# Branch projections in three rounded passes, branch by branch, and a first expert tile in fp32

## The reference

```python
# h: normalised and modulated tokens; gates: the last 3 * 1024 columns of h @ w_in
g_f, g_g, g_d = jnp.split(jax.nn.sigmoid(gates), N_BRANCHES, axis=-1)
merged = (g_f * (fourier_mix(u_f) @ w_f)      # w_fourier (512, 1024)
          + g_g * (o_g @ w_go)                # w_gqa_o   (512, 1024)
          + g_d * (o_d @ w_do))               # w_diff_o  (512, 1024)
x = x + g1 * (merged @ w_out)
...
# moe: 16 experts, two per token; t: tokens after the second norm
gate = jnp.einsum('td,edf->tef', t, w_gate_l)
up = jnp.einsum('td,edf->tef', t, w_up_l)
act = jax.nn.silu(gate) * up * combine[..., None]
x = x + g2 * jnp.einsum('tef,efd->td', act, w_down_l)
```

## Time and profile before

| | |
|---|---|
| median of 3 runs | 2156.6 us (2156.22 to 2162.78) |
| the profiled execution, its own time | 2155.64 us |
| its span, first to last instruction | 2153.8 us, 30419 instructions |
| granted TensorE clock, mean | 0.964 |
| TensorE matmul | 1965.9 us busy, 91% of the span |
| TensorE weight load (beside it) | 1611.4 us, 75% |
| VectorE | 1025.5 us, 48% |
| ScalarE | 850.0 us, 39% |
| GpSimd | 340.8 us, 16% |
| DMA | 336.28 MB, 156 GB/s on average |

### The profile page before, as it was taken

How to read it: one execution, slowest core, us unless ns; L and a number is a source line. 1 busy time by engine, 2 the same in 40 slices (tenths; PEclk the granted TensorE clock), 3 DMA queues, 4 the chain that set the end, 5 groups by cost and what they waited for, 6 DMA issues and landing times. The chain is left out here.

```text
span 2153.8 us, 30419 instructions
## 1 busy us (share of the span) xinstructions
PE 1965.9 (91%) x12363; PEld 1611.4 (75%) x12363; DVE 1025.5 (48%) x1718; ACT 850.0 (39%) x1377; POOL 340.8 (16%) x131
## 2 busy tenths in 40 slices
PE   6999899999999969999679997878999998799994
PEld 5889766688888856676478995657888887677673
DVE  5384367511122266777564733672221123677763
ACT  4333455511111235565334334654111123366553
POOL 1223000013222220000222221000222230200003
PEclk9999999999999989999889998999999999899997
DMA  7312378628211159899431220001212112899954
GB/s 268 107 59 61 129 245 262 209 88 303 88 59 56 58 200 342 305 313 313 168 114 41 69 70 31 2 1 51 77 59 88 59 45 98 322 408 389 313 204 170
DMA packets 163853, 336.28 MB, mean 156 GB/s; under 512 B 10370, under 2 KB 121602, under 8 KB 149252
## 3 DMA queue, kind: packets, MB, share of 16 engines
q1 hardware_dynamic: 151488, 299.63, 40.1%
q0 software_dynamic: 5760, 20.97, 2.6%
q10 hardware_dynamic: 6468, 13.74, 1.8%
HBM read 334.58 MB, written 53.74 MB: 180 GB/s over the span
## 5 line engine op out<-in xcount | busy, mean ns | idle before, releaser
L653 POOL TENSOR_TENSOR wlo<-raw,whi 128x2048 fp32r<-128x2048 f32 x50 | 230.4, 4608 | 1075.5 <-ACT whi L676 1075.5
L1729 DVE TENSOR_TENSOR xw_gu_lo<-xw_gu_raw,xw_gu_hi 128x2048 fp32r<-128x2048 f32 x100 | 228.0, 2283 | 26.7 <-ACT xw_gu_hi L1515 26.6
L170 PE MATMUL psum<-h_hi,whi 128*128 128x320 f32 x896 | 217.1, 324 | 20.4 <-DVE h_lo L155 17.7
L170 PE MATMUL psum<-whi,h_hi 128*128 128x256 f32 x720 | 212.4, 295 | 0.0
L170 PE MATMUL psum<-wlo,h_hi 128*128 128x256 f32 x720 | 206.2, 286 | 0.0
L170 PE MATMUL psum<-whi,h_lo 128*128 128x256 f32 x720 | 206.2, 286 | 0.0
L170 PE MATMUL psum<-h_lo,whi 128*128 128x320 f32 x896 | 205.2, 310 | 0.0
L170 PE MATMUL psum<-h_hi,wlo 128*128 128x320 f32 x896 | 205.0, 310 | 0.0
L833 ACT ACTIVATE sig_m<-psum 128x640 f32<-128x640 f32 x48 | 33.8, 705 | 400.0 <-PE psum L170 400.0
L1515 ACT ACTIVATE xw_gu_hi<-xw_gu_raw 128x2048 fp32r<-128x2048 f32 x100 | 185.5, 1907 | 0.0
L1868 PE MATMUL psum<-xw_d_raw,act_T 128*128 128x512 f32 x400 | 179.9, 592 | 0.9 <-ACT act_T L1541 0.9
(11 more groups left out here) (288 smaller groups left out, 3463.4 us busy)
## 6 DMA issues: line engine op xcount, KB each, us to landing
xw_gu_raw<-w_e_gate SPq DMA_DIRECT2D x50, 1024.0 KB
xw_gu_raw<-w_e_up SPq DMA_DIRECT2D x50, 1024.0 KB
xw_d_raw<-w_e_down SPq DMA_DIRECT2D x50, 1024.0 KB, 9.8
raw<-w_in SPq DMA_DIRECT2D x46, 1024.0 KB, 5.4
wm_rest<-w_mod SPq DMA_DIRECT2D x40, 1024.0 KB, 5.2
y_rows<-y_sel SPq DMA_DIRECT2D x50, 512.0 KB, 9.6
h_sel<-h_rows SPq DMA_DIRECT2D x48, 512.0 KB, 8.2
h_rows<-c_zero ACTq DMA_DIRECT2D x1, 12800.0 KB, 47.5
```

Source lines behind the costliest of these rows:

```text
L170: mm = pe.matmul(dst, st, mv[q], start=start and n == 0, stop=stop and n == 2)
L653: pool.tensor_tensor(wlo[i % 2][:, :, :], raw[i % 2][:, :, :], whi[i % 2][:, :, :].bitcast(F32), ALU.subtract).then_inc(w_lo, 1)
L1729: dve.tensor_tensor(gu_lo[i % 2][:, n, :, :], gu_raw[i % 2][:, n, :, :], gu_hi[i % 2][:, n, :, :].bitcast(F32), ALU.subtract).then_inc(x_l ...
```

## The change

It has two parts. **Branch products.** The weights `pw` are split into `pw_hi` (ScalarE) and `pw_lo` (VectorE), the branch rows into `branch_hi` (ScalarE) and `branch_lo` (VectorE, in place of the rows), and a branch block becomes 24 three-pass matmuls. The twelve chunks go branch by branch, n = 4 b + m, so that each branch's rows are split once and their room can be used again; the eight sums of 128 output columns are kept until the last branch (`mg_acc`), and split in chunks 8 to 11. The clearing of `h_rows` stays in chunk 2. The first two gate blocks now run back to back, with `turn_diff` behind them and before the first branch block. **First expert tile.** Its gate and up weights are loaded into a buffer of their own (`gu_first`), after the last branch block, and used as loaded in 8 fp32 matmuls with rows copied whole (`h_first`). The rows of tiles 1 and 2 are gathered ahead of tile 2's weights, VectorE's subtractions for tile 1 wait for the scatter, and the order of tiles 0 to 2 is written out.

```diff
+        mg_acc = at("mg_sum", [P, KD, TOK], M + 50 * K)
+        branch_raw = (y_T[:, :, :], q_T[:, 0:4, :], q_T[:, 4:8, :])
+        branch_hi = [at(f"branch_hi{b}", [P, 4, TOK], off, F32R) for b, off in enumerate((M + 30 * K, M + 40 * K, M))]
+        branch_lo = [at(f"branch_lo{b}", [P, 4, TOK], M + 10 * K * b, F32R) for b in range(3)]
+        pw_lo = [at(f"pw_lo{i}", [P, 4, WC], M - 8 * K + 4 * K * i, F32R) for i in range(2)]
+        pw_hi = [at(f"pw_hi{i}", [P, 4, WC], M + (60, 64, 80, 84)[i] * K, F32R) for i in range(4)]
...
+                    for n in range(12):
+                        lo(N_WIN + n + 2)
+                        for fc in range(2 if n >= 8 else 0):
+                            f = 2 * (n - 8) + fc
+                            pool.wait_ge(g_hi, f + 1)
+                            pool.tensor_tensor(mg_lo[:, f, :], mg_acc[:, f, :], mg_hi[:, f, :].bitcast(F32), ALU.subtract).then_inc(g_lo, 1)
...
+                    def pw_high(n):
+                        act.wait_ge(p_ld[n % 2], 16 * (n // 2 + 1))
+                        if n >= 4:
+                            act.wait_ge(g_pfull, 2 * (n - 1))
+                        act.activation(pw_hi_of(n)[:, :, :], pw[n % 2][:, :, :], ACT.Copy).then_inc(p_hi, 1)
...
+                    def pw_low(n):
+                        dve.wait_ge(p_hi, n + 1)
+                        dve.tensor_tensor(pw_lo[n % 2][:, :, :], pw[n % 2][:, :, :], pw_hi_of(n)[:, :, :].bitcast(F32),
+                                          ALU.subtract).then_inc(p_lo, 1)
...
-                                for kc in range(4):
-                                    for hf in range(2):
-                                        mm = pe.matmul(pair(2 + g % 2)[:, hf, 0:HALF], pw[n_p % 2][:, kc, fc * P:(fc + 1) * P],
-                                                       branch[b][:, kc, hf * HALF:(hf + 1) * HALF],
-                                                       start=(kc == 0), stop=(kc == 3))
+                        pe.wait_ge(p_lo, n + 1)
+                        pe.wait_ge(b_lo, b + 1)
+                        if g >= 2:
+                            pe.wait_ge(g_pfree, g - 1)
+                        dst = pair(2 + g % 2)
+                        for kc in range(4):
+                            mm = mm_split(pe, [dst[:, 0, 0:HALF], dst[:, 1, 0:HALF]], pw_hi_of(n)[:, kc, cs], pw_lo[n % 2][:, kc, cs],
...
+                    gate(0)
+                    gate(1)
+                    turn_diff()
+                    branch(0)
+                    branch(1)
...
-                    sp.wait_ge(w_lo, N_STREAM - ahead)
+                    sp.wait_ge(g_pfree, 24)
                     load_gate_up(0)
                     sp.wait_ge(o_full, KD)
                     load_gate_up(1)
                     load_down(0)
+                    sp.wait_ge(w_lo, N_STREAM - ahead)
+                    sp.wait_ge(gu_ld[0], 32)
+                    sp.wait_ge(r_st, IDX_STEPS)
                     sp.wait_ge(k_s, 16 * 2 * TT)
                     load_h(1)
-                    sp.wait_ge(r_st, IDX_STEPS)
+                    load_h(2)
+                    load_gate_up(2)
...
-                    lo(0, "g")
-                    h_low(0)
-                    lo(0, "u")
+                    dve.wait_ge(k_s, 16 * 2 * TT)
                     lo(1, "g")
                     lo(1, "u")
                     activated(0)
                     h_low(1)
...
+                    def gate_up_first():
+                        pe.wait_ge(x_hh, 1)
+                        pe.wait_ge(gu_ld[0], 32)
+                        for kc in range(KD):
+                            mm = pe.matmul(psum[:, 0, :], h_first[:, kc, :], gu_first[:, :, kc, :], start=(kc == 0), stop=(kc == KD - 1))
+                        mm.then_inc(x_gu, 1)
```

More of the change, by code:

```diff
@@ new lines, in _ @@
+                    for n in range(12):
+                        b, m = divmod(n, 4)
+                        for fc in range(2):
+                            g = 2 * n + fc
+                            f = 2 * m + fc
+                            dve.wait_ge(g_sig, g + 1)
+                            dve.wait_ge(g_pfull, g + 1)
+                            src = pair(2 + g % 2)[:, :, 0:HALF]
+                            sg = sig_m[:, g % 2, :].rearrange("p (a b) -> p a b", a=2)
+                            dst = mg_acc[:, f, :] if b == 0 else mg_t[:, :]
+                            dve.tensor_tensor(dst.rearrange("p (a b) -> p a b", a=2), src, sg, ALU.mult).then_inc(g_pfree, 1)
+                            if b > 0:
+                                dve.wait_ge(g_pfree, g + 1)
+                                dve.tensor_tensor(mg_acc[:, f, :], mg_acc[:, f, :], mg_t[:, :], ALU.add).then_inc(g_acc, 1)
+                                n_acc += 1
+                                dve.wait_ge(g_acc, n_acc)
+                        if n + 1 < 12:
+                            pw_low(n + 1)
+                        if n in (1, 5):
+                            branch_low(1 if n == 1 else 2)
@@ L1363, in route_sums @@
+                    pe.wait_ge(w_lo, N_WIN + 1 - ahead)
+                    gate(0)
[3 more added lines that the diff above has]
+                    branch(1)
+                    for n in range(1, 12):
+                        pe.wait_ge(w_lo, N_WIN + n + 1 - ahead)
+                        for fc in range(2):
+                            gate(2 * n + fc)
+                            branch(2 * n + fc)
                     def route_sums(f):
@@ L1760, in _ @@
                     h_low(1)
-                    for i in range(1, N_TILES):
-                        if i >= 2:
-                            keep_y(i - 2)
+                    lo(2, "g")
+                    lo(2, "u")
+                    activated(1)
+                    h_low(2)
+                    for i in range(2, N_TILES):
+                        keep_y(i - 2)
                         if i + 1 < N_TILES:
@@ L1886, in _ @@
                     mm.then_inc(x_th, 1)
-                    for i in range(N_TILES):
-                        if i >= 1:
-                            turn_act(i - 1)
-                        if i == 0:
-                            gate_up(0)
-                            turn_h(1)
-                            continue
+                    gate_up_first()
+                    turn_h(1)
+                    turn_act(0)
+                    gate_up(1)
+                    turn_h(2)
+                    down(0)
+                    for i in range(2, N_TILES):
+                        turn_act(i - 1)
                         if i + 1 < N_TILES:
```

188 lines of the change are left out of this document (89 added, 99 removed).

## The result

| | before | change |
|---|---|---|
| median of the runs, us | 2156.41 (2153.97 to 2162.78, 4 runs) | 2132.78 (2130.46 to 2133.33, 4 runs) |
| ratio | | 0.9884, 95% interval 0.9871 to 0.9897 |
| profiled execution, own time / span, us | 2155.64 / 2153.8 | 2130.46 / 2128.6 |

Faster by 23.6 us in the medians (1.2%, and the interval excludes no change) and by 25.2 in the profiled executions, where 38.3 were forecast. The sign was right; the time lies 1.8 us above the range (2106 to 2131).

A forecast was written before the change was run, and what follows sets the result against it. TensorE was taken to bound the branch stage and, except at its start, the expert stage. Terms -36.4 + 6.3 + 0.5 + 5.4 - 1.6 - 7.5 - 5 gave -38.3 us, forecast 2118.0 us, range 2106 to 2131.

The forecast's parts named there:

- the blocks: Branch stage: a block of 24 rounded products takes 3.52 us in place of 4.31, for both layers -36.4 us.
- no wait for pw_lo in chunks 5 to 8: Branch stage, b = 1: VectorE's pw_lo ready about 0.3 us before TensorE wants it, costing nothing, 2.4 us at most.
- pw_lo late in b = 2: Chunks 9 to 11: pw_lo ends S+11.4 (S: start of the chunk's second sigmoid), 1.05 us late, six times, +6.3 us.
- Rival (b): VectorE wins the port shared with GpSimd: the +6.3 goes and the end gains 1.4 more, 2110 us; chance 0.12.
- rival (e): Branch stage: each wait for pw_lo could cost TensorE its clock, half rate for 3 us after, 2222 us; chance 0.03.
- (a): Layer 0: the load of pw(4) isn't late, arriving by 510, so +5.4 becomes -1.4, 2111 us; chance 0.15.
- (d): Branch stage: pw_lo late in every chunk of b = 1, later in b = 2, both loads late, up to 2130; chance 0.13.
- (c): Experts: the DMA engines eat the gain, -3 us in place of -12.5, 2127 us; chance 0.12.
- 6.8 us of waiting for the 1.4 now, +5.4: Layer 0, branch stage: the load of pw(4), due earlier, arrives late beside the clearing of h_rows, costing +5.4 us.
- the copy ends at 793.03 and 8 fp32 products start: First expert tile, layer 0: picked product ends 791.98, copy follows, products take 7.7 us; part of the experts' -7.5.
- the gathered rows leave 1.5 to 2.6 us before 799.70: Layer 0's experts: with VectorE waiting for the scatter, the gathered rows are issued sooner and arrive at 801.1.
- the rows ahead of the weights: Experts, layer 0: tile 2's rows issued ahead of its 2 MB of weights, so TensorE's wait of 6.37 us goes.

The follow-up runs named there:

- e5: Changed kernel with h_rows cleared after the last branch block, plus VectorE making pw_lo ahead of the chunk's last addition: 2114.35 us, ratio 0.9798 to the kernel before.
- e7: Changed kernel with GpSimd's scatter of h_tok held back until the picked product is done: 2148.25 us (one run).
- e9: e5 with VectorE's subtraction for tile 1's gate weights ahead of its wait for the scatter: 2111.60 us, ratio 0.9785 to the kernel before.
- e10: e5 with both VectorE subtractions for tile 1 ahead of its wait for the scatter: 2113.17 us, ratio 0.9792 to the kernel before.
- e11: e5 with the rows of tile 2 issued behind its gate and up weights, no longer ahead: 2112.50 us, ratio 0.9794 to the kernel before.
- e1: The branch part of the change alone, on the experts of before: 2138.83 us, ratio 0.9910 to the kernel before.
- e6: Changed kernel with a semaphore counted up by each of the other 39 matmuls of the picked product: 2132.61 us (one run).
- e2: The first expert tile and its loads alone, on the branch stage of before: 2151.76 us, ratio 0.9962 to the kernel before.
- e8: e5 run again, on the same chip as e9 and e10: 2112.39 us, ratio 0.9795 to the kernel before.

## Why the prediction was right or wrong

- **Right: the blocks.** 3.53 us each, no wait for pw_lo in chunks 5 to 8 of either layer. There it ends at 545.59, 0.26 before TensorE wants it; 0.3 was forecast.
- **Right: pw_lo late in b = 2.** S+11.36 where S+11.4 was worked out, 7.0 us for 6.3. e5 shows the mechanism by taking it away. Rival (b), VectorE always first, falls.
- **Right: short waits don't cost the clock** (rival (e)). Three waits of 0.9 us left it at 1.00 through layer 1's stage.
- **The other rivals.** (a) falls, since the load took 28.7 us. Of (d), pw_lo was late in no chunk of b = 1. (c) put the experts' gain at 3 us for 12.5: by the means above both layers together gave 6.4, which lies between it and the forecast; what held them is told below.
- **Wrong size: "6.8 us of waiting for the 1.4 now, +5.4".** The wait was 8.05. The load took 1.1 longer than before; TensorE came 1.4 later than forecast, and the request, which hangs on the same blocks, 1.3 later. More than the wait itself, the 3.0 us at half clock behind it were missing, though rival (e) quotes the very rows in which a pause of 5.38 is followed by a clock of 0.50. The term was +9.4.
- **Wrong step: "the copy ends at 793.03 and 8 fp32 products start".** That the copy begins when the product is done was taken for granted. It began 3.87 and 3.66 us late, and behind that pause the 8 products took 9.34 and 9.72 at a clock partly at half, where 7.7 was forecast and 7.13 is what they take at full clock (e7, e9). e7 shows that both hang on the scatter. The forecast had noticed that VectorE now waits for the scatter, and counted it as a gain only. The loss is bounded by e9 and e10: without the late signal the experts gain 2 us in all, in the traces, since the gathered rows are due next. What the fp32 tile itself is worth against three passes with the new loads wasn't tried.
- **Wrong step: "the gathered rows leave 1.5 to 2.6 us before 799.70".** Counted from the scatter's start they left 1.0 us earlier in layer 0 and not at all in layer 1 (17.55 us for 17.54). The forecast took the scatter to be as much shorter as its calls. In layer 0 its last call now ends 14.7 us after its start for 17.3 before, but the DMA engines were at 0.98 behind the picked product, and the request didn't follow. In e7, where all calls but the first take 0.95 us and the last ends after 12.5, it still comes 16.5 us after the start. That is why an earlier signal is worth so little.
- **Wrong reason: the rows ahead of the weights** (e11), with no effect on the sum.
- **Not in the sum, and no fault of its mechanism: 4.4 us in stretches left alone**, of which the one in the routing shows as a lower clock. The profiled execution of before had short ones: the profiles of e1 to e11 are longer in layer 1's attention by 0.4 to 2.4 us. It had long experts, too (277.7 us for 274.8 in e1), so that the table gives the experts more than they gained. A sum against one execution carries such errors.

What beats both kernels is e9, at 0.9785 of before (0.9766 to 0.9804), or e5, from which it can't be told: the change, less its late load and its wait for the port.

## What to carry to other kernels

Price a wait of TensorE of several microseconds with its clock: here 8.05 us cost 11.0 and a pause of 4.9 cost 2.2 to 2.6 more, while waits of 0.9 us left the clock alone. When a change makes an operand due earlier, look for bulk transfers in the gap (12.8 MB of zeros could go 200 us later), and put the one subtraction that someone waits for first among those that share a lock. Before paying for a shorter start of a stage, ask what else arrives at its end.

## What the runs showed of the hardware

- While GpSimd's scatter calls followed each other at 0.95 us, with the DMA engines at 0.9 to 0.99, TensorE's semaphore signals came out in pairs, 1.4 us apart (e6), and the last one of the product came 3.5 to 4.8 us late, 0.1 to 1.8 us behind the end of the last call, in all 16 layers in which VectorE stood idle beside the scatter's end and the product's (the changed kernel, e2 to e6, e8, e11). With the scatter behind the product it was 0.3. The records of the matmuls don't show it: they run at full pace to the end. With loads from SyncE's queue at 1.02 of the DMA engines no signal of TensorE came over 0.61 us behind the start of its record. Which part of the chip holds them stays open.
- The Trainium skill ("SBUF — State Buffer", section "SBUF: two separate sides") describes how VectorE can keep GpSimd from writing descriptors, as a trap. The rows agree that a call beside a subtraction of VectorE is held up (2.06 us for 0.95), but here TensorE's signals came only 0.3 to 0.8 us late beside such a slowed call in e9, though 3.1 in layer 1 of e1.
